# Holding the gating layer's first z weights in an idle buffer, and running a second u and z pair ahead of the last spatial product

## The chip, the cores and the metric

The kernel runs on the 8 cores of one Trainium2 chip. Each core has its own prompt stream of 4096 frames and four of the 32 sample streams; the cores exchange nothing and run the same program. The metric is the device time in microseconds (us) of the slowest core. TensorE multiplies, VectorE (DVE) and ScalarE (ACT) work on elements and bring results out of PSUM, GpSimd (POOL) does a few copies, and SyncE (SP) issues nearly all DMA transfers, in the order of its queue.

## What is computed

The reference is a trunk of four layers over rows of 1024 numbers, with an inner width of 2048:

```python
for i in range(DEPTH):                       # kinds 0, 1, 2, 0
    h = rmsnorm(x, norm_g[i])
    if kind == 0:   # pooling mixer on u, then (y * silu(z)) @ pool_out_w
        ...
    elif kind == 1: # GLU, causal depthwise convolution of width 31, layernorm, silu
        ...
    else:
        p = h @ sgu_in_w[j]                                    # (B,T,3E)
        u, v, z = p[..., :D_INNER], p[..., D_INNER:2 * D_INNER], p[..., 2 * D_INNER:]
        y, st = sgu_mixer(u, v, sgu_w[j], sgu_b[j], sgu_norm_g[j], sgu_norm_b[j])
        out = (y * jax.nn.silu(z)) @ sgu_out_w[j]
    x = x + out
```

The third layer, the gating layer, is the one that changes. Its mixer normalises v (layernorm over the 2048 channels), multiplies it along the 128 positions of a chunk by a lower-triangular matrix of each of four heads (the *spatial product*), adds a bias, and multiplies by u.

## The kernel before

Each core walks through eight groups (g = 0 to 7) of 512 prompt frames. In the even groups 32 frames of a sample stream come along, so that a group has 544 columns. Activations lie with channels on partitions and frames along the row, in bf16 for TensorE (`h`, `ym`) and in f32 for the residual. In a group the four layers follow one another: L0 (pooling), L1 (convolution), L2 (gating), L3 (pooling).

**Weights.** A pass over the layers uses 112 chunks of 128 x 2048 bf16 (512 KB). They stream through nine buffers, `slots`: chunk `gi` lies in slot `gi % 9`. `use_chunk` issues loads on SyncE up to six chunks ahead. In group 0 a chunk comes from `wst` as f32 (1 MB) through one of two staging buffers `stg` (L238), is converted on ScalarE (L240) and stored by ScalarE's queue in `wq` (L244); later groups load it from `wq` (L269). In an input projection one chunk holds the columns of two output tiles, `m2` = 0 and 1.

**Order.** The order of instructions on every engine is that in which the program adds them (`S.add`); semaphores are worked out from what each reads and writes. So a DMA on SyncE or a conversion on ScalarE that has to wait holds up all that was added to that engine behind it.

**The gating layer.** Its chunks are 8 of v (offsets 0 to 7 from 56), then u and z in turn: chunk 8 is u's first, 9 z's first (the diff calls it `L2 + 9`), 10 u's second, and so on, then 8 of the output projection. The eight v chunks stay in their slots until the last block of frames is done; with chunk 8 all nine slots are full, so chunk 9 takes the slot of the first v chunk. The frames go in blocks of 128 (four, and a fifth of 32 sample frames in even groups). For a block, `vstage` runs the v projection (L1050) into four PSUM banks; ScalarE brings it out (L1062); DVE takes statistics (L1067, L1070); two small ScalarE steps and two DVE steps make scale and shift (L1072 to L1081); ScalarE normalises (L1085). In the sample block, and in the last block of g = 7, L1090 normalises once more in f32 for the output, and in the sample block SyncE stores that in `svn` (L1096). `sstage` runs the spatial product (L1108, 16 matmuls, four to a head, each head in a bank of its own); DVE evicts three heads (L1133, four instructions each) and ScalarE the fourth (L1119). The loop is `vstage(t+1)`, `sstage(t)`.

Ahead of the last `sstage` stand early projections that `pre_tile` makes (L554): in even groups the u tile of channel tile 0, in odd groups its u and z tiles. PSUM has eight banks; a tile is two banks in even groups and one in odd groups; `vtiles` lists the eight in the order of the ring, the spatial product uses the first four, the early tiles the next ones. Then, for the 16 channel tiles, come the rest of u and z (L382), each z through Silu on ScalarE (L1225), two DVE products (L1228, L1231) and so into `ym` for the output projection (L484, L382, residual added at L500).

**The buffer.** `wdt` (three parts of 128 x 1024 bf16) holds the diagonal matrices of the convolution in L1, and in group 0 and in the last group some data of the pooling layers. In L2 nothing uses it. `L433` makes the row scale for the next layer; in L2 of group 0 DVE also works out `bt`, the bias of the spatial product (L1153), once.

## Time and profile before

| | us |
|---|---|
| median of 3 runs (4903.69 to 5186.77) | 4910.05 |
| the profiled execution | 4896.68 |
| its span, first to last instruction, slowest core (core 5) | 4895.1 |
| TensorE busy in it | 3990.6 (82%) |
| DVE, ScalarE, GpSimd busy | 2111.9, 1860.0, 648.3 |
| spans of the eight cores | 4868.6 to 4895.1 |
| granted TensorE clock, mean of a core | 0.928 to 0.933 |

"Busy" counts time in which at least one instruction of the engine was at work. The granted clock is the share of full speed (2.4 GHz) that TensorE was given; it is 0.5 or 1.0 at any moment. Shapes in a row read partitions x elements. All rows are of core 5. A row's figure in brackets is the idle time of the engine just before it, and behind the arrow what ended it.

### The profile page before, as it was taken

To read this page: it belongs to the slowest core of one execution; us is meant where nothing else is said; L and a number is where in the kernel's file an instruction comes from. 1 tells how busy PE (TensorE), PEld (TensorE's weight loads), DVE (VectorE), ACT (ScalarE), POOL (GpSimd) and SP (SyncE) were. 2 spreads that over 40 slices of the span, in tenths; PEclk is the share of its full clock that TensorE was granted. 3 is DMA by queue.
4 is the path that set the end of the run, shared out by engine and by line. 5 is a ranking of instruction groups with operands and counts; after the bars stand their busy time and mean duration, and the time that the engine had idled before them with its cause. 6 is when DMAs were issued, how large, how long until landed. Compare 5 with 4: busy or idle time off the path is not lost.

```text
span 4895.1 us, 88633 instructions; the slowest of 8 cores (4868.6 to 4895.1 us)
## 1 busy us (share of the span) xinstructions
PE 3990.6 (82%) x30572; PEld 2529.7 (52%) x30572; DVE 2111.9 (43%) x4227; ACT 1860.0 (38%) x3353; POOL 648.3 (13%) x931
## 2 busy tenths in 40 slices
PE   3845657778899878998899878997899878978886
PEld 1533445533345757753446657753446667733443
DVE  2411333542347334552457234552556234542444
ACT  3522645432434244332534243331524243332523
POOL 1111000211002210112002200212012200202000
PEclk8977879989999999999999999999999999999999
DMA  6754547645345543445254643446254633446353
GB/s 192 259 176 142 202 160 272 231 149 157 116 152 167 141 124 103 143 152 155 93 184 156 149 118 102 142 153 161 104 171 156 152 102 112 138 181 162 112 178 140
DMA packets 320997, 752.98 MB, mean 154 GB/s; under 512 B 85680, under 2 KB 171056, under 8 KB 302512
## 3 DMA queue, kind: packets, MB, share of 16 engines
q1 hardware_dynamic: 304432, 688.59, 45.7%
q10 hardware_dynamic: 16128, 58.73, 2.9%
q8 instruction: 254, 4.16, 0.4%
q14 instruction: 183, 1.50, 0.1%
HBM read 647.62 MB, written 99.56 MB: 153 GB/s over the span
## 4 chain that ended last, share of the span: by engine, by line
PE 65%; DVE 10%; ACT 9%; DMA 8%; issue 7%; SPq 1%; ACTq 1%; POOL 0%; DVEq 0%; POOLq 0%
PE ps L382 45%; DMA stg<-wst 6%; PE ps L837 5%; PE ps L484 5%; DVE h L453 3%; ACT slots L240 2%; PE ps L554 2%; ACT t L858 2%; PE ps L1050 2%; PE ps L421 1%; PE ps L1009 1%; PE ps L394 1%; PE ps L865 1%; DVE big L1133 1%; DVE big L847 1%
## 5 line engine op out<-in xcount | busy, mean ns | idle before, releaser
L382 PE MATMUL ps<-h,slots 128*128 128x272 bf16 (+1 forms) x12448 | 1964.8, 319 | 171.5 <-ACT t L880 48.4
L382 PEld LDWEIGHTS ps<-h,slots 128*128 128x128 bf16 x12448 | 1230.8, 100 | 874.3 <-issue 251.6
L382 PE MATMUL ps<-ym,slots 128*128 128x272 bf16 (+1 forms) x4352 | 671.9, 313 | 16.3 <-DVE x L500 16.3
L382 PEld LDWEIGHTS ps<-ym,slots 128*128 128x128 bf16 x4352 | 430.4, 99 | 231.1 <-issue 27.2
L806 POOL TENSOR_TENSOR wdt<-par,bc 128x1024 bf16<-128x1024 f32 x128 | 244.5, 1910 | 1075.1 <-PE ps L837 656.5
L654 ACT ACTIVATE scr<-ps,par 128x272 f32<-128x272 f32 (+3 forms) x495 | 209.7, 477 | 302.7 <-PE ps L382 158.9
L484 PE MATMUL ps<-ym,slots 128*128 128x272 bf16 (+1 forms) x1792 | 291.8, 323 | 12.2 <-DVE t L1228 7.3
L847 DVE TENSOR_SCALAR big<-ps,par 128x276 f32<-128x276 f32 (+1 forms) x192 | 106.8, 584 | 445.9 <-PE ps L837 445.9
L776 DVE TENSOR_TENSOR agb<-ps,t 128x272 bf16<-128x272 f32 (+3 forms) x256 | 98.7, 429 | 449.7 <-ACT t L762 439.7
L837 PE MATMUL ps<-ym,wdt 128*32 128x276 bf16 (+2 forms) x6144 | 271.5, 328 | 16.5 <-DMA ym<-asc 16.1
L762 ACT ACTIVATE t<-ps 128x272 f32<-128x272 f32 (+1 forms) x164 | 69.4, 458 | 565.5 <-PE ps L382 556.5
L865 PE MATMUL ps<-t,ones_e 128*128 128x272 bf16 (+1 forms) x192 | 50.9, 320 | 283.3 <-ACT t L858 283.3
L240 ACT ACTIVATE slots<-stg 128x2048 bf16<-128x2048 f32 x96 | 183.4, 1911 | 205.0 <-DMA stg<-wst 184.9
L500 DVE TENSOR_TENSOR x<-ps,x 128x272 f32<-128x272 f32 x256 | 99.2, 436 | 345.6 <-PE ps L382 285.1
L484 PEld LDWEIGHTS ps<-ym,slots 128*128 128x128 bf16 x1792 | 175.7, 98 | 123.8 <-issue 15.5
L1228 DVE TENSOR_TENSOR t<-ps,t 128x272 f32<-128x272 f32 (+1 forms) x192 | 94.9, 522 | 335.1 <-ACT t L1225 335.1
L1225 ACT ACTIVATE t<-ps 128x272 f32<-128x272 f32 (+1 forms) x192 | 82.2, 462 | 366.7 <-PE ps L382 364.9
L837 PEld LDWEIGHTS ps<-ym,wdt 128*32 128x32 bf16 x6144 | 165.2, 100 | 107.8 <-issue 59.3
L500 DVE TENSOR_TENSOR stg<-ps,stg 128x512 f32<-128x512 f32 x128 | 84.9, 689 | 315.1 <-PE ps L382 226.7
L602 POOL COPY scr<-pool_hp 128x15 f32<-128x15 f32 x256 | 130.5, 511 | 612.6 <-DVE t L706 348.6
L1050 PE MATMUL ps<-slots,scr 128*128 128x256 bf16 (+1 forms) x1792 | 210.4, 280 | 0.0
L631 ACT ACTIVATE big<-ps 128x272 f32<-128x272 f32 (+1 forms) x362 | 154.7, 464 | 145.2 <-PE ps L382 137.4
(132 smaller groups left out, 4422.3 us busy)
## 6 DMA issues: line engine op xcount, KB each, us to landing
slots<-wq SPq DMA_DIRECT2D x784, 512.0 KB, 4.3
stg<-wst SPq DMA_DIRECT2D x120, 1024.0 KB, 7.2
ym<-asc SPq DMA_DIRECT2D x512, 129.8 KB, 3.6
wq<-slots ACTq DMA_DIRECT2D x112, 512.0 KB, 7.1
asc<-agb SPq DMA_DIRECT2D x128, 128.0 KB, 3.7
yT<-big SPq DMA_DIRECT2D x64, 256.0 KB, 2.2
x<-wun SPq DMA_DIRECT2D x16, 1024.0 KB, 5.9
x<-xT SPq DMA_DIRECT2D x32, 256.0 KB, 5.7
```

Of the source, the lines that this page charges most:

```text
L240: S.add("act", lambda e, st=st, out_ap=out_ap: e.activation(out=out_ap, in_=stg[:, st, :], func=AF.Copy), reads=[("stg", st)], writes=out_ ...
L382: inst = e.matmul(psap(tile, bi, n), lhsT=lhs_fn(k), rhs=rhs_fn(k, c0, n), start=(k == 0), stop=(k == nk - 1))
L453: S.add("dve", lambda e, k=k: e.scalar_tensor_tensor(out=h[:, k, a:T], in0=XAP(G, k, a, T - a), scalar=par[:, g0 + k: g0 + k + 1], in1=rs[ ...
L484: inst = e.matmul(psap(tile, bi, n), lhsT=slots[:, sl, k * 128:(k + 1) * 128], rhs=ym[:, k, c0:c0 + n], start=(ki == 0), stop=(ki == 15))
L500: blockwise("dve", G, lambda e, bi, c0, n, m=m, tile=tile: e.tensor_tensor(out=XAP(G, m, c0, n), in0=psap(tile, bi, n), in1=XAP(G, m, c0, ...
L602: S.add("pool", lambda e: e.tensor_copy(out=seqb[:, p, 0:H], in_=pool_hp[:, j, ct, :]), reads=[("pool_hp", j, ct)], writes=[("seqb", p)])
L631: blockwise("act", G, lambda e, bi, c0, n, ct=ct, tile=tile: e.activation(out=big[:, ct, c0:c0 + n], in_=psap(tile, bi, n), func=AF.Silu), ...
L654: inst = e.activation(out=seqb[:, p, so:so + ln], in_=psap(tile, bi, ln, off=lo - c0), func=AF.Copy, scale=par[:, P_PSCALE + j * 16 + ct:P ...
L806: S.add("pool", lambda e, w2=w2, wc=wc: e.tensor_tensor(out=wdt[:, w2, :].rearrange("p (a b) -> p a b", b=32), in0=wc.unsqueeze(2).broadca ...
L837: inst = e.matmul(psap(tile, bi, n, p0=32 * gq, p1=32 * gq + 32), lhsT=wdt[:, w2, (gq * 8 + k) * 32:(gq * 8 + k) * 32 + 32], rhs=ash[b][:, ...
L847: inst = e.tensor_scalar(out=big[:, ct, c0:c0 + n], in0=psap(tile, bi, n), scalar1=par[:, P_CONVB + ct:P_CONVB + ct + 1], scalar2=None, op ...
L1050: inst = e.matmul(psap(tile, bi, 256, p0=0, p1=nt, off=c2 * 256), lhsT=xg[:, k, tok0:tok0 + nt], rhs=slots[:, slv[cc], k * 256:(k + 1) * 256],
```

## The change

Chunk `L2 + 9`, z's first, no longer takes a slot but the first two parts of `wdt`; so it can be loaded while all eight v chunks are held. Its slot stays empty for that turn. `use_chunk` may run one chunk further ahead while the v chunks are held. Ahead of the last spatial product there are now u and z of channel tile 0 in even groups (banks 6 and 7 serve the z tile), and u and z of channel tiles 0 and 1 in odd groups. Behind it the ring of PSUM tiles starts again at `vt0` in both.

```diff
+    def slot_of(gi):
+        return NSLOT if gi % NCH == L2 + 9 else gi % NSLOT
+
+    def SLOT(sl):
+        return slots[:, sl, :] if sl < NSLOT else wdt2d[:, 0:2048]
+
+    def SLK(sl):
+        return [("slot", sl)] if sl < NSLOT else [("wdt", 0), ("wdt", 1)]
...
     def use_chunk(gi, hold_from=None):
         upto = min(gi + PF, total_chunks - 1)
         if hold_from is not None:
-            upto = min(upto, hold_from + NSLOT - 1)
+            upto = min(upto, hold_from + NSLOT - 1 + (hold_from % NCH == L2))
...
             if tci == nch - 1:
                 table(AF.Silu)
-                if even:
-                    mk, rd, tile = pre_tile(G, gbase + cbase + 8, 0, tuple(q[0] for q in vtiles[4:6]), h)
-                    upre["u"] = tile
+                units = [(0, "u"), (0, "z")] if even else [(0, "u"), (0, "z"), (1, "u"), (1, "z")]
+                for q, (c, nmz) in enumerate(units):
+                    tile = tuple(b[0] for b in vtiles[4 + 2 * q:6 + 2 * q]) if even else vtiles[4 + q]
+                    mk, rd, tile = pre_tile(G, gbase + cbase + (8 if nmz == "u" else 9), c, tile, h)
+                    upre[nmz, c] = tile
                     S.add("pe", lambda e, mk=mk: mk(e, range(8)), reads=rd + HALL, writes=[*PK(tile)])
-                else:
-                    for q, nmz in ((4, "u"), (5, "z")):
-                        mk, rd, tile = pre_tile(G, gbase + cbase + (8 if nmz == "u" else 9), 0, vtiles[q], h)
-                        upre[nmz] = tile
-                        S.add("pe", lambda e, mk=mk: mk(e, range(8)), reads=rd + HALL, writes=[*PK(tile)])
-                    nxt_tile = (vt0 + 6) % len(G["tiles"])
                 state["tile"] = 0
             sstage(tci)
-        state["tile"] = vt0 if even else nxt_tile
+        state["tile"] = vt0
...
-                if ct == 0:
-                    tU = upre["u"]
+                if ("u", ct) in upre:
+                    tU = upre["u", ct]
```

All other places that read or write a slot by its number go through `SLOT` and `SLK`. The early tiles show in the order of the engines. TensorE in group 0, the end of the gating layer's loop, before and now; the line numbers of the changed kernel are higher by 9 (1108 is 1117, 554 is 563, 382 is 391):

```order
L1050 MATMUL ps<-slots,scr 32x256 x64
L1108 MATMUL ps<-wmT,ym 128x128 x16
L554 MATMUL ps<-h,slots 128x272 x16
L1108 MATMUL ps<-wmT,dbuf 128x32 x16
L382 MATMUL ps<-h,slots 128x272 x496
```

```order
L1059 MATMUL ps<-slots,scr 32x256 x64
L1117 MATMUL ps<-wmT,ym 128x128 x16
L563 MATMUL ps<-h,slots 128x272 x16
L563 MATMUL ps<-h,wdt 128x272 x16
L1117 MATMUL ps<-wmT,dbuf 128x32 x16
L391 MATMUL ps<-h,slots 128x272 x16
L391 MATMUL ps<-h,wdt 128x272 x16
L391 MATMUL ps<-h,slots 128x272 x448
```

The z tile of channel tile 0 has moved in front of the last 16 small products, and the z tiles of channel tiles 0 and 1, both from chunk 9, now read `wdt`. In group 1, without a sample block, the same place before and now:

```order
L1108 MATMUL ps<-wmT,ym 128x128 x16
L554 MATMUL ps<-h,slots 128x512 x16
L1108 MATMUL ps<-wmT,dbuf 128x128 x16
L382 MATMUL ps<-h,slots 128x512 x240
L484 MATMUL ps<-ym,slots 128x512 x48
```

```order
L1117 MATMUL ps<-wmT,dbuf 128x128 x16
L1059 MATMUL ps<-slots,scr 128x256 x64
L1117 MATMUL ps<-wmT,ym 128x128 x16
L563 MATMUL ps<-h,slots 128x512 x8
L563 MATMUL ps<-h,wdt 128x512 x8
L563 MATMUL ps<-h,slots 128x512 x8
L563 MATMUL ps<-h,wdt 128x512 x8
L1117 MATMUL ps<-wmT,dbuf 128x128 x16
```

Sixteen more matmuls stand in front of the last products, and 224 instead of 240 behind them. ScalarE in group 0, where the row scale for the gating layer is made (L433, now L442), before and now:

```order
L240 ACTIVATE slots<-stg 128x2048
L244 DMA wq<-slots 128x2048
L433 ACTIVATE rs<-ps,epsb 128x272 x2
L436 ACTIVATE rs<-rs 128x544
L1062 ACTIVATE vraw<-ps 128x512 x4
```

```order
L240 ACTIVATE slots<-stg 128x2048
L253 DMA wq<-slots 128x2048
L240 ACTIVATE wdt<-stg 128x2048
L253 DMA wq<-wdt 128x2048
L442 ACTIVATE rs<-ps,epsb 128x272 x2
L445 ACTIVATE rs<-rs 128x544
L1071 ACTIVATE vraw<-ps 128x512 x4
```

The conversion of z's first chunk has moved here, in front of the row scale, from behind the eviction of the last spatial product. On SyncE, in group 2, the load has moved in front of the store of `svn`; before and now:

```order
L988 DMA o_convs<-cso 128x480
L269 DMA slots<-wq 128x2048 x11
L1096 DMA svn<-vraw 32x2048
L269 DMA slots<-wq 128x2048 x31
L1296 DMA stg<-xT 128x512 x8
```

```order
L997 DMA o_convs<-cso 128x480
L278 DMA slots<-wq 128x2048 x11
L278 DMA wdt<-wq 128x2048
L1105 DMA svn<-vraw 32x2048
L278 DMA slots<-wq 128x2048 x30
L1301 DMA stg<-xT 128x512 x8
```

Of the 31 chunk loads behind the store 30 are left, u's second chunk first among them.

## Rows read from the trace of the kernel before

**Rows 1.** The page: busy time of TensorE, and the chain that ended last.
```profile
PE 3990.6 (82%) x30572; PEld 2529.7 (52%) x30572; DVE 2111.9 (43%) x4227; ACT 1860.0 (38%) x3353; POOL 648.3 (13%) x931
...
PE 65%; DVE 10%; ACT 9%; DMA 8%; issue 7%; SPq 1%; ACTq 1%; POOL 0%; DVEq 0%; POOLq 0%
```

**Rows 2.** Timeline, g = 2: start, duration (us), engine, line, instruction, count, [idle before].
```profile
1910.45 1.07 PE L1108 MATMUL ps<-wmT,ym 128*128 128x128 bf16 x16
1911.37 2.01 PE L554 MATMUL ps<-h,slots 128*128 128x272 bf16 x16
...
1917.22 2.09 ACT L1090 ACTIVATE vraw<-vraw,mv 32x2048 f32<-32x2048 f32 x1
...
1917.38 0.39 PE L1108 MATMUL ps<-wmT,dbuf 32*128 32x32 bf16 x8 [4.00 <-ACT dbuf L1085]
...
1920.42 11.63 SPq L269 DMA_DIRECT2D slots<-wq  x9
...
1920.46 0.26 PE L1108 MATMUL ps<-wmT,dbuf 32*128 32x32 bf16 x4 [1.96 <-ACT big L1119]
...
1925.03 7.21 PE L382 MATMUL ps<-h,slots 128*128 128x272 bf16 x37 [4.31 <-DMA slots<-wq]
```

**Rows 3.** Windows, g = 2: PE, PEld, DVE, ACT, POOL busy; clock, DMA, GB/s.
```profile
1917.30:1920.70 3.40, 0.89 (x16) 0.68 (x16) 2.69 (x16) 3.38 (x6) 0.24 (x1) 0.50 0.18 39
...
1925.00:1930.70 5.70, 5.67 (x26) 3.71 (x27) 0.89 (x3) 0.69 (x2) 0.00 (x0) 0.50 1.01 398
...
1937.00:1987.00 50.00, 49.68 (x417) 39.61 (x415) 19.69 (x39) 8.91 (x26) 0.00 (x0) 1.00 0.41 130
```

**Rows 4.** Timeline of ScalarE, g = 2: the Silu of z0, z1 and z2.
```profile
1928.91 0.69 ACT L1225 ACTIVATE t<-ps 128x272 f32<-128x272 f32 x2 [6.03 <-PE ps L382]
1933.61 0.69 ACT L1225 ACTIVATE t<-ps 128x272 f32<-128x272 f32 x2 [4.01 <-PE ps L382]
1937.45 0.69 ACT L1225 ACTIVATE t<-ps 128x272 f32<-128x272 f32 x2 [3.15 <-PE ps L382]
```

**Rows 5.** Timeline, g = 1.
```profile
1371.67 3.62 PE L554 MATMUL ps<-h,slots 128*128 128x512 bf16 x16
...
1375.08 6.29 DVE L1133 SCALAR_TENSOR_TENSOR big<-ps,par,bt 128x128 f32<-128x128 f32 x24
...
1377.57 1.85 PE L1108 MATMUL ps<-wmT,dbuf 128*128 128x128 bf16 x16 [2.29 <-ACT dbuf L1085]
...
1379.22 11.06 PE L382 MATMUL ps<-h,slots 128*128 128x512 bf16 x46
...
1383.90 0.60 ACT L1225 ACTIVATE t<-ps 128x512 f32<-128x512 f32 x1 [2.45 <-PE ps L382]
```

**Rows 6.** Windows, g = 1, columns as in rows 3.
```profile
1377.50:1381.20 3.70, 3.63 (x21) 2.21 (x22) 3.70 (x15) 3.67 (x11) 1.27 (x2) 0.54 0.03 7
```

**Rows 7.** Timeline and one window, g = 7.
```profile
4663.58 0.59 PE L1108 MATMUL ps<-wmT,dbuf 128*128 128x128 bf16 x4 [1.70 <-ACT big L1119]
...
4669.78 0.60 ACT L1225 ACTIVATE t<-ps 128x512 f32<-128x512 f32 x1 [3.24 <-PE ps L382]
...
4661.40:4668.20 6.80, 5.10 (x18) 2.09 (x18) 4.25 (x14) 5.11 (x12) 2.37 (x2) 0.50 0.00 0
```

**Rows 8.** Timeline, g = 0: ScalarE and DVE at the row scale, TensorE later on.
```profile
626.35 0.87 ACT L433 ACTIVATE rs<-ps,epsb 128x272 f32<-128x272 f32 x2 [0.51 <-PE ps L421]
...
631.83 2.06 ACT L1062 ACTIVATE vraw<-ps 128x512 f32<-128x512 f32 x4 [3.87 <-PE ps L1009]
...
632.07 4.23 DVE L1153 SCALAR_TENSOR_TENSOR bt<-ps,par,bc 128x128 f32<-128x128 f32 x16 [29.62 <-PE ps L1144]
...
715.55 3.68 PE L382 MATMUL ps<-h,slots 128*128 128x272 bf16 x16 [20.02 <-ACT big L1119]
...
754.19 7.70 PE L382 MATMUL ps<-h,slots 128*128 128x272 bf16 x64 [1.75 <-DVE t L1228]
```

**Rows 9.** DMA issues from 682.5 to 791.9: count, size, median us to landing.
```profile
stg<-wst SPq DMA_DIRECT2D x23, 1024.0 KB, 7.6
```

More of the change, by code:

```diff
@@ L241, in raw_load @@
               reads=[("stg", st)], writes=out_keys)
+    def slot_of(gi):
[4 more added lines that the diff above has]
+        return [("slot", sl)] if sl < NSLOT else [("wdt", 0), ("wdt", 1)]
     def store_chunk(ci, sl):
-        S.add("act", lambda e, ci=ci, sl=sl: [e.dma_start(out=wq[ci], in_=slots[:, sl, :])],
-              reads=[("slot", sl)], writes=[("wq", ci)], dkey=("slot", sl))
+        S.add("act", lambda e, ci=ci, sl=sl: [e.dma_start(out=wq[ci], in_=SLOT(sl))],
+              reads=SLK(sl), writes=[("wq", ci)], dkey=("slot", sl))
     def pool_part(ci):
@@ L255, in issue_load @@
         grp = gi // NCH
-        sl = gi % NSLOT
+        sl = slot_of(gi)
         if grp == 0:
@@ L265, in issue_load @@
                 idx = ci + 4 if ci < L3 else 92 + ci - L3 + 4
-            raw_load(idx, slots[:, sl, :], [("slot", sl)])
+            raw_load(idx, SLOT(sl), SLK(sl))
             store_chunk(ci, sl)
         else:
-            S.add("sp", lambda e, ci=ci, sl=sl: [e.dma_start(out=slots[:, sl, :], in_=wq[ci])],
-                  reads=[("wq", ci)], writes=[("slot", sl)], dkey=("slot", sl))
+            S.add("sp", lambda e, ci=ci, sl=sl: [e.dma_start(out=SLOT(sl), in_=wq[ci])],
+                  reads=[("wq", ci)], writes=SLK(sl), dkey=("slot", sl))
     def raw_issue(j, gq):
@@ L368, in use_chunk @@
             state["loaded"] += 1
-        return gi % NSLOT
+        return slot_of(gi)
     L0 = 0
@@ L393, in fn @@
                     for bi, (c0, n) in enumerate(G["blocks"]):
-                        inst = e.matmul(psap(tile, bi, n), lhsT=slots[:, sl, k * 256 + m2 * 128: k * 256 + m2 * 128 + 128],
+                        inst = e.matmul(psap(tile, bi, n), lhsT=SLOT(sl)[:, k * 256 + m2 * 128: k * 256 + m2 * 128 + 128],
                                         rhs=h[:, k, c0:c0 + n], start=(k == 0), stop=(k == 7))
                     return inst
-                S.add("pe", fn, reads=[("slot", sl), *HKEY(k)], writes=[*PK(tile)])
+                S.add("pe", fn, reads=SLK(sl) + HKEY(k), writes=[*PK(tile)])
             return
         mm_tile(G, tile, 8,
-                lambda k: slots[:, sl, k * 256 + m2 * 128: k * 256 + m2 * 128 + 128],
+                lambda k: SLOT(sl)[:, k * 256 + m2 * 128: k * 256 + m2 * 128 + 128],
                 lambda k, c0, n: h[:, k, c0:c0 + n],
-                reads=[("slot", sl)] + HALL)
+                reads=SLK(sl) + HALL)
     def blockwise(eng, G, fn_block, reads, writes):
@@ L553, in mk @@
                 for bi, (c0, n) in enumerate(G["blocks"]):
-                    inst = e.matmul(psap(tile, bi, n), lhsT=slots[:, sl, k * 256 + m2 * 128: k * 256 + m2 * 128 + 128],
+                    inst = e.matmul(psap(tile, bi, n), lhsT=SLOT(sl)[:, k * 256 + m2 * 128: k * 256 + m2 * 128 + 128],
                                     rhs=src[:, k, c0:c0 + n], start=(k == 0), stop=(k == 7))
             return inst
-        return mk, [("slot", sl)], tile
+        return mk, SLK(sl), tile
     def ps_scale(G, out_fn, tile, writes, scalar=None):
@@ L1217, in sgu_layer @@
                     inproj(G, slu, m2, tU)
-                if ct == 0 and "z" in upre:
-                    tZ = upre["z"]
+                if ("z", ct) in upre:
+                    tZ = upre["z", ct]
                 else:
```

## The prediction

> **What bounds the kernel now.** I read the page first. TensorE is busy for 3990.6 of 4895.1 us, 82%; no other engine passes 43% [rows 1]. The chain that ended last is TensorE for 65% of the span, by far the largest part of it L382, the input and output projections. So a microsecond in which TensorE stands idle is worth about a microsecond, as long as the work that it is waiting to do is on the chain. The change acts at one place of each of the eight groups: around the last spatial product (L1108) of the gating layer and the u and z projections (L382) behind it. So the next view was the timeline there, for each kind of group, and the windows, for the granted clock.
>
> A group with a sample block (g = 2, 4, 6; shown g = 2) [rows 2]. TensorE ends the early u tile (L554) at 1913.38 and is idle 4.00 us, until ScalarE has normalised the last v block (L1085). Its sixteen small products then dribble until 1920.73: the last four wait 1.96 us for an eviction (L1119) which on ScalarE stands behind L1090, 2.09 us that make the output copy of v. Then it is idle again, 4.31 us, until a weight chunk lands. Why so late: SyncE works its queue in order, the store of `svn` waits for L1090, and all weight chunks from z0 on stand behind that store; they go out at 1920.42. From 1917.3 to 1930.7 the clock is at 0.50, behind that at 1.00 (shown from 1937.0 on) [rows 3]. ScalarE's Silu gives the ends of the z tiles: z0's at 1928.91, z1's at 1933.61, z2's at 1937.45 [rows 4]. The first tile, 1925.03 to 1928.91, took 3.88 us at half clock; the last two, 1933.61 to 1937.45, took 3.84 together, so a tile of 16 matmuls costs 1.92 at full clock.
>
> A group without one (g = 1, 3, 5; shown g = 1) [rows 5]. The early u and z tiles take 3.62 us together; then 2.29 idle for the normalised block; the sixteen products last until 1379.4; L382 follows at once, at 1379.22. No load is waited for. u1 and z1 end when the Silu starts at 1383.90. From 1377.5 to 1381.2 the clock is at 0.54, half speed but for an edge [rows 6].
>
> The last group (g = 7) is like it, but the last products also wait 1.70 us for the eviction behind L1090, L382 starts right behind them, at 4664.0, and its first two tiles end at 4669.78; the clock is 0.50 up to 4668.2 [rows 7].
>
> Group 0 loads weights as f32, 1 MB each at 7.6 us from issue to landing, converts each on ScalarE (L240) and stores it. Six conversions stand on ScalarE in front of the eviction of the last spatial product, and TensorE waits 20.02 us for it. From there on L382 stands still for 1.8 to 3.6 us in each round of four tiles (7.70 us), always because the Silu stands behind conversions that wait for a landing [rows 8, 9]. That stretch is bound by the stream of loads: 23 of them in the 109.4 us from 682.5 to 791.9, 4.76 us each.
>
> **The change, part by part.**
>
> *The buffer.* z's first chunk goes to `wdt`, whose last readers, the diagonals' matmuls, ended in the layer before; it is issued in front of `svn`, with some 45 us to go, where the others take 4.3 us. No bytes are added and no wait falls on TensorE. What is queued behind it: on SyncE the `svn` store, far off. In group 0 its conversion and store stand on ScalarE in front of L433, which makes the scale of the rows. L433 now starts at 626.35, right behind a conversion. One more load cannot start before a staging buffer is free, some 4 us before that; it lands 7.6 later, near 630, and the conversion is another 2, so L433 starts near 632. Who waits: L1169 on TensorE and L1062 on ScalarE, which stands at 631.83 after 3.87 idle, so becomes late by up to 2 us. Behind it the statistics on DVE wait anyway, as DVE is busy with `bt` until 636.30 [rows 8]. I cost this at 0; without that cover it is 2 us, once.
>
> *Sample groups, three of them.* z0 (1.92) moves into the 4.00 idle in front of the products, which start when they did. Behind them u1 and z1 need no landing, since a chunk holds two tiles' columns and both chunks are there; they start at 1920.73, not 1925.03. Their PSUM: u1 takes two banks that DVE evicts; z1's second bank is evicted by ScalarE (1.1 us, behind L1090 and a table load), while u1 runs. What is late next is the chunk of u2, now first in the line at 1920.42: landed at 1925.0, as z0's was. u1 and z1 cost 3.84 at full clock and 7.76 at half. The idle is shorter by nearly 6 us, so full clock comes back earlier. I take u1 at half (ends 1924.6) and z1 between the two (2.9, ends 1927.5). Before, z1 ended at 1933.6. Gain 6.1. Bounds: all at full clock, u2 begins at the landing, 1925.0, gain 8.6; half clock right to 1930.7, both end at 1928.5 and u2's next 2.2 us count half, which leaves 5.1 - 1.1 = 4.0; and 1 us more for a second chunk that is not there in time, 3.0. Three groups: 18.3 (9 to 25.8).
>
> *Groups without sample, three.* The second pair costs 3.62 and begins at 1375.29, so it ends at 1378.9; the products could have begun at 1377.57. They are 1.3 late and no longer wait for evictions, so they take 1.07 as where nothing hinders them [rows 2] and not 1.85: they end at 1380.0. New wait: u2 now takes the bank that the first of them wrote, not one that is free. Four evictions of 0.27 each on DVE from 1379.3 make it free at 1380.4. Before, u2 began at 1383.9. Gain 3.5 with full clock throughout. If the half clock comes as it did, from 1377.5 to 1381.2, it lies on 1.4 us of the pair, 1.07 of products and the start of u2, which costs up to 1.8: gain 1.7. I take 2.7 (the nearer row is one with 2.29 idle ahead; here some 0.4 is left). Three groups: 8.1 (5.1 to 10.5).
>
> *The last group.* The pair ends at 4661.8 or 4662.0, the products still wait for the eviction, until 4663.58, and u2 starts at 4664.2 instead of 4669.78. At half clock until 4668.2 it does 2.0 us less than at full: gain 5.4 down to 3.4; I take 4.3.
>
> *Group 0.* One load leaves the bound stretch: the six conversions in front of the eviction are those of the next six chunks, and one fewer follows. u1 runs early where z0 did; what starts at 715.55 is z1 and no longer u1. Worth one place of the stream, 4.76; I take 5, from 3 (later idle swallows some) to 7 (the first Silu no longer stands behind a seventh conversion).
>
> *PSUM order.* The ring of tiles is a place or two further on in each later stage. A tile at a change of ring then meets a bank used one or two turns earlier or later; at some 0.4 us for an eviction and a few such places per group I cost it at 0, within 3 us either way.
>
> Sum: 18.3 + 8.1 + 4.3 + 5 = 35.7 us less; from 9 + 5.1 + 3.4 + 3 = 20.5 to 25.8 + 10.5 + 5.4 + 7 = 48.7. The profiled execution took 4896.68, 1.6 beside its span, so it would be 4861.0. The other runs gave 4903.69, 4910.05 and 5186.77; the last is 5.6% off the rest and left out. The middle of the three that are left is 4903.69, and I forecast from that: 4868.
>
> **A rule weighed against a row.** Sixteen matmuls of 512 columns took 3.62 us, 226 ns each [rows 5]. By the Trainium skill ("TensorE: Matmul & The Clock Gate", Back-to-back issue gap) a stream of weight load and matmul settles near 131 ns at that size. By that figure, an estimate, the second pair would be 2.1 us, hide wholly in the 2.29 idle, and be worth 2.1 in such a group in place of my 2.7, so 1.8 less in the sum. The row decides.
>
> **The rivals.**
> (a) *The clock no longer falls.* For it: the half clock comes each time behind an idle stretch and ends after TensorE has been busy [rows 3, 6]; idle goes from 4.0 + 2.4 + 4.3 to about 2.0 + 2.4 in sample groups and from 2.29 to near 0.4 in the others. Against: the products themselves are thin (0.89 busy of 3.40), and in sample groups they still dribble. It gives the upper end, 48.7: 4855. The same page (Part 1) calls the throttled state the default that activity releases; the rows agree as far as they go.
> (b) *The gain is only half there*, because u1 and z1 meet another wait in the place of the old: half clock to its old end, the second chunk late, the odd groups' idle filled but the products late. The lower end, 20.5, or a little less: 4885.
> (c) *It ends slower.* TensorE works on more, and thinner, stretches of full and half clock: the pair in front, run just before a fall, no longer keeps the clock up behind the products, so a fall comes a second time in L382. One fall as that of rows 7 (0.50 up to 4668.2 from 4661.4) costs 3.4 us of work. Two more in each of eight groups cost 54, against 35.7 gained: 18 slower, 4922. It decides from 4.5 us lost per group. Against it: behind the products L382 was busy 49.68 of 50 us at 1.00 [rows 3], and nothing in it is thinned.
> (d) *It does not do what it says*: the early chunk is there, but TensorE is not what the end hangs on and the time comes back in a later stage. Against: 65% of the chain is TensorE. Nearly no change, 4900.
>
> **How the numbers follow.** Forecast as summed: 0.55, time 4868 (4858 to 4880). (a) 0.17, 4855. (b) 0.18, 4885. (c) 0.04. (d) 0.06. The range 4845 to 4892 takes in the forecast, (a), (b) and the 0.15% by which those three runs differ from their middle; it leaves out (c), (d) and some spill. 2% of this kernel is 98 us, about what a measurement can tell from no change; no case but a gross surprise reaches it. Faster by over 2%: 0.02; within: 0.95; slower: 0.03.
>
> **What would show it.** Right: in g = 2 no wait of L382 for `slots<-wq` over 0.5 us, L382 from 1920.7 on in that group's time, the products at the same distance from the last v matmuls as before; in g = 1 idle before the products near 0 and a wait of a few tenths for L1133 before u2; in g = 0 L433 some 5 us later and L382 to its end about 5 us sooner. Wrong: the products of g = 2 start later than their normalised block, L382 waits for a chunk at u2 or z2, or the half clock lasts as long behind L382's start as it did (5.7 us). What would make the forecast wrong most of all is the clock, since each fall more or less in a group is worth 1.7 to 3.4 us.

## The result, and the profile after

The changed kernel against the kernel before, run in turn on one chip: ratio 0.9936, 95% interval 0.992 to 0.9952, so 0.64% less time (0.48 to 0.80%). The forecast, 4868 against a middle of 4903.69, was 0.73% less. The median of all six timed runs is 4951.43 us (4868.80 to 5087.15), outside the forecast range of 4845 to 4892, and that of the kernel before 5048.41 (4903.69 to 5494.93): both are pulled up by runs in which the four cores of a die had a lower granted clock than the others, as in the 5186.77 that the prediction left out, and such runs, and in the profiles below such cores, are left out of every comparison. The other three runs of the changed kernel gave 4868.80, 4875.14 and 4883.44, inside that range, those of the kernel before 4903.69, 4905.57 and 4910.05. Their middles are 30.4 us apart; 35.7 were forecast. The profiled execution took 4875.14, against 4896.68.

The page of the changed kernel, the lines that answer to [rows 1]:

```profile
PE 3986.7 (82%) x30377; PEld 2537.2 (52%) x30572; DVE 2111.5 (43%) x4227; ACT 1858.5 (38%) x3353; POOL 647.4 (13%) x931
...
PE 66%; DVE 9%; ACT 9%; DMA 7%; issue 7%; SPq 1%; ACTq 1%; POOL 0%; DVEq 0%; another core or an unknown queue 0%; POOLq 0%
```

Nothing else has become the bound. All rows from here on are of core 5 where no other is named, and every line number is higher by 9 (by 5 behind L1200). The timeline of g = 2, TensorE and SyncE, which answers to [rows 2]:

```profile
1886.83 1.07 PE L1117 MATMUL ps<-wmT,ym 128*128 128x128 bf16 x16
1887.74 2.01 PE L563 MATMUL ps<-h,slots 128*128 128x272 bf16 x16
1889.60 2.02 PE L563 MATMUL ps<-h,wdt 128*128 128x272 bf16 x16
1893.76 0.37 PE L1117 MATMUL ps<-wmT,dbuf 32*128 32x32 bf16 x8 [2.15 <-ACT dbuf L1094]
...
1896.84 0.26 PE L1117 MATMUL ps<-wmT,dbuf 32*128 32x32 bf16 x4 [1.97 <-ACT big L1128]
1897.07 3.49 PE L391 MATMUL ps<-h,slots 128*128 128x272 bf16 x16
1900.40 2.02 PE L391 MATMUL ps<-h,wdt 128*128 128x272 bf16 x16
1902.25 4.00 PE L391 MATMUL ps<-h,slots 128*128 128x272 bf16 x32
...
1896.80 4.65 SPq L278 DMA_DIRECT2D slots<-wq  x9
```

From the early u tile to L391 it was 13.66 us (1911.37 to 1925.03); it is 9.33 (1887.74 to 1897.07), with one tile more done in it. The idle in front of the products has shrunk from 4.00 to 2.15, as they now wait behind a z tile; the 1.96 for the eviction has stayed; the 4.31 for the chunk is gone. u1 takes 3.3 us, z1 1.9, and the loads that now go out at 1896.80 are there when u2 needs them.

The windows, which answer to [rows 3] and [rows 6]:

```profile
1893.50:1897.00 3.50, 0.78 (x16) 0.66 (x16) 2.87 (x16) 3.39 (x7) 0.16 (x1) 0.96 0.18 42
1897.00:1901.00 4.00, 4.00 (x26) 2.82 (x23) 0.95 (x3) 2.60 (x8) 1.44 (x2) 0.61 0.90 297
1901.00:1906.00 5.00, 5.00 (x45) 4.05 (x43) 2.08 (x4) 0.69 (x2) 0.00 (x0) 1.00 1.03 418
1359.60:1408.10 48.50, 48.48 (x225) 22.03 (x226) 22.43 (x38) 9.66 (x19) 1.18 (x1) 1.00 0.46 141
```

The clock (the last figure but two) fell at 1917.3 before, at the start of the products, and came back between 1930.7 and 1937. Now it holds until the last four of them (0.96 over the stretch), falls there and is back at 1.00 by 1901, 4 us after L391 began. The last row is the whole of L391 in g = 1: never below full speed. The timeline that answers to [rows 5], g = 1:

```profile
1350.94 1.89 PE L563 MATMUL ps<-h,slots 128*128 128x512 bf16 x8
...
1356.12 1.89 PE L563 MATMUL ps<-h,wdt 128*128 128x512 bf16 x8
1357.85 1.06 PE L1117 MATMUL ps<-wmT,dbuf 128*128 128x128 bf16 x16
1359.62 4.69 PE L391 MATMUL ps<-h,slots 128*128 128x512 bf16 x21 [0.71 <-DVE big L1142]
```

Four early tiles fill the wait for the normalised block; the products take 1.06 and are not waited for. u2 waits 0.71 for the bank that the first product wrote. It starts 8.7 us behind the first early tile; before, that was 12.2 [rows 5]. In g = 7 the last products still wait for the eviction behind the second normalisation, 1.27 us in place of 1.70 [rows 7]:

```profile
4617.18 0.83 PE L1117 MATMUL ps<-wmT,dbuf 128*128 128x128 bf16 x12
4619.28 0.38 PE L1117 MATMUL ps<-wmT,dbuf 128*128 128x128 bf16 x4 [1.27 <-ACT big L1128]
4619.52 6.85 PE L391 MATMUL ps<-h,slots 128*128 128x512 bf16 x31
```

Group 0, ScalarE, DVE and TensorE, against [rows 8]:

```profile
621.08 1.91 ACT L240 ACTIVATE wdt<-stg 128x2048 bf16<-128x2048 f32 x1 [4.55 <-DMA stg<-wst]
623.49 0.87 ACT L442 ACTIVATE rs<-ps,epsb 128x272 f32<-128x272 f32 x2 [0.51 <-ACT wdt L240]
...
621.96 4.23 DVE L1162 SCALAR_TENSOR_TENSOR bt<-ps,par,bc 128x128 f32<-128x128 f32 x16 [26.42 <-PE ps L1153]
...
626.95 2.47 DVE L1076 BATCH_NORM_STATS2 bst<-vraw 128x6 f32<-128x512 f32 x4
...
625.25 1.17 PE L1178 MATMUL ps<-epsb,rs 1*128 1x1 f32 x10 [3.40 <-ACT rs L445]
...
681.57 2.01 PE L391 MATMUL ps<-h,slots 128*128 128x272 bf16 x16 [1.31 <-DVE big L1142]
704.31 3.78 PE L391 MATMUL ps<-h,wdt 128*128 128x272 bf16 x16 [20.73 <-ACT big L1128]
```

**The ledger.** To see where the time went I cut each trace into stages, from the first TensorE instruction of one to the first of the next, and took the mean over the cores. The gating layer from its v projection to the start of its output projection, after less before, in us; "forecast" are the terms of the prediction:

| group | 0 | 1 | 2 | 3 | 4 | 5 | 6 | 7 | sum |
|---|---|---|---|---|---|---|---|---|---|
| measured | -5.6 | -2.8 | -6.5 | -3.0 | -6.4 | -3.2 | -5.7 | -5.5 | -38.8 |
| forecast | -5 | -2.7 | -6.1 | -2.7 | -6.1 | -2.7 | -6.1 | -4.3 | -35.7 |

In g = 0 the cores lie far apart (159.5 to 170.0 us for the changed kernel), so its -5.6 is good to some 2.6 us; the others agree far better. All that lies outside these stages came out 11 us longer in this pair of traces. That was not forecast, and some of the experiments are on it. For them I also split a stage's loss in two: TensorE's idle, and its half-speed loss, which is half of the time that it was busy at 1.2 GHz. The gating layer's -38.9 is idle 137.7 to 108.7 (-29.0) and half-speed loss 39.6 to 30.1 (-9.5). The rest: idle 713.7 to 710.7, half-speed loss 149.2 to 164.8.

### The profile page after: what moved, and what is told of

Its sections match the earlier page's. It is cut to its first block, busy times and chain, and to the rows that moved or that the text cites. A ratio compares the mean times of both kernels' runs of the same rounds, so it can differ in the third digit from the quotient of the medians.

```text
span 4873.6 us, 88400 instructions; the slowest of 8 cores (4839.0 to 4873.6 us)
## 1 busy us (share of the span) xinstructions
PE 3986.7 (82%) x30377; PEld 2537.2 (52%) x30572; DVE 2111.5 (43%) x4227; ACT 1858.5 (38%) x3353; POOL 647.4 (13%) x931
## 4 chain that ended last, share of the span: by engine, by line
PE 66%; DVE 9%; ACT 9%; DMA 7%; issue 7%; SPq 1%; ACTq 1%; POOL 0%; DVEq 0%; another core or an unknown queue 0%; POOLq 0%
PE ps L391 45%; DMA stg<-wst 6%; PE ps L846 5%; PE ps L493 5%; DVE h L462 3%; PE ps L563 2%; ACT slots L240 2%; PE ps L1059 2%; ACT t L867 2%; PE ps L403 1%; PE ps L430 1%; PE ps L1018 1%; PE ps L874 1%; DVE big L1142 1%; DVE big L856 1%
## 5 line engine op out<-in xcount | busy, mean ns | idle before, releaser
L391 PE MATMUL ps<-h,slots 128*128 128x272 bf16 (+1 forms) x12154 | 1929.3, 319 | 168.0 <-ACT t L889 48.2
L391 PEld LDWEIGHTS ps<-h,slots 128*128 128x128 bf16 x12256 | 1213.3, 100 | 829.2 <-issue 213.7
L391 PE MATMUL ps<-ym,slots 128*128 128x272 bf16 (+1 forms) x4327 | 674.3, 313 | 18.3 <-DVE x L509 16.6
L391 PEld LDWEIGHTS ps<-ym,slots 128*128 128x128 bf16 x4352 | 431.7, 99 | 235.1 <-issue 33.2
L771 ACT ACTIVATE t<-ps 128x272 f32<-128x272 f32 (+1 forms) x164 | 69.4, 458 | 572.6 <-PE ps L391 561.9
L681 POOL COPY pool_hp<-scr 128x15 f32<-128x15 f32 x224 | 143.4, 640 | 509.8 <-ACT scr L663 487.5
```

Of the source, the lines that this page charges most:

```text
L391: inst = e.matmul(psap(tile, bi, n), lhsT=lhs_fn(k), rhs=rhs_fn(k, c0, n), start=(k == 0), stop=(k == nk - 1))
L681: S.add("pool", lambda e, p=p, ct=ct: e.tensor_copy(out=pool_hp[:, j, ct, :], in_=seqb[:, p, 512:512 + H]), reads=[("seqb", p)], writes=[( ...
```

## The experiments

Ratios are to the kernel before, from runs in turn on the same chip. "Gating" is the ledger's sum for the gating layer.

**1 and 2: the parts alone.** The buffer, with the early tiles of before, and in the odd groups the place in the ring of before:

```diff
-                units = [(0, "u"), (0, "z")] if even else [(0, "u"), (0, "z"), (1, "u"), (1, "z")]
+                units = [(0, "u")] if even else [(0, "u"), (0, "z")]
...
-        state["tile"] = vt0
+        state["tile"] = vt0 if even else (vt0 + 6) % len(G["tiles"])
```

> The changed kernel with the buffer and the earlier load kept, and the early tiles as they were before (u0 in sample groups, u0 and z0 in the others). Times are of the gating layer (start of its v projection to start of its output projection on TensorE, mean of the cores) against the kernel before; the whole change measured -6.5, -6.4, -5.7 in g = 2, 4, 6; -2.8, -3.0, -3.2 in g = 1, 3, 5; -5.5 in g = 7; -5.6 in g = 0. Theory 1, the gain of a sample group has two parts, the landing that z0 no longer waits for (4.3 idle, less what half clock takes) and z0's 1.9 in the idle ahead of the products: here -4 in each of g = 2, 4, 6, 0 in g = 1, 3, 5, 7 (no load was waited for there), -5 in g = 0 (one load fewer in the bound stretch), -17 in all. Theory 2, the early tiles are the gain and the buffer is only what makes them possible, since z0 without them meets unfinished evictions: -1 at most in sample groups, 0 elsewhere, -3 in all. Theory 3, in g = 0 the load stream is not what counts: 0 there.

And chunk 9 back in its slot, even groups as before, four early tiles in odd ones:

```diff
     def slot_of(gi):
-        return NSLOT if gi % NCH == L2 + 9 else gi % NSLOT
+        return gi % NSLOT
...
-            upto = min(upto, hold_from + NSLOT - 1 + (hold_from % NCH == L2))
+            upto = min(upto, hold_from + NSLOT - 1)
...
-                units = [(0, "u"), (0, "z")] if even else [(0, "u"), (0, "z"), (1, "u"), (1, "z")]
+                units = [(0, "u")] if even else [(0, "u"), (0, "z"), (1, "u"), (1, "z")]
```

> No buffer; z0 in its slot as before; sample groups as before; in the odd groups four early tiles (u0, z0, u1, z1) instead of two. Gating layer against the kernel before, mean of the cores. Theory 1, the odd groups gain by the second pair in the idle ahead of the products alone and need no buffer: -3 in g = 1, 3, 5, -5.5 in g = 7, 0 in the even ones, -14.5 in all. Theory 2, in the odd groups too the earlier load counts: less than half of that.

The buffer alone: 0.996 (0.9943 to 0.9976). Gating: g = 2, 4, 6: -4.4, -4.7, -3.9; g = 0: -7.8; odd groups 0 within 0.3; sum -21.1. Its timeline in g = 2:

```profile
1899.16 2.01 PE L563 MATMUL ps<-h,slots 128*128 128x272 bf16 x16 [0.25 <-ACT vraw L1071]
1905.18 0.39 PE L1117 MATMUL ps<-wmT,dbuf 32*128 32x32 bf16 x8 [4.01 <-ACT dbuf L1094]
...
1908.59 3.71 PE L391 MATMUL ps<-h,wdt 128*128 128x272 bf16 x16
```

The idle of 4 us in front of the products is that of before; L391 follows them without a landing. The odd pair alone: 0.998 (0.9967 to 0.9992); g = 1, 3, 5, 7: -2.8, -2.9, -3.0, -5.1; g = 2, 4, 6 within 0.5; g = 0: -1.6; sum -16.1. So the odd groups owe nothing to the buffer and the sample groups two thirds of theirs; the last third, -6.2 less -4.3, is the z tile moved into the idle.

**3 and 4: what the load waited for.** The `svn` store put on SyncE behind the loads for the early tiles, in the changed kernel (3) and in the kernel before (4), where it is the only edit:

```diff
-                    S.add("sp", lambda e, s=s, VR=VR: [e.dma_start(out=svn[s], in_=VR[0:32, :])],
-                          reads=VK, writes=[("svn",)], dkey=("vraw", bs))
+                    late.append(lambda s=s, VR=VR, VK=VK, bs=bs: S.add(
+                        "sp", lambda e: [e.dma_start(out=svn[s], in_=VR[0:32, :])],
+                        reads=VK, writes=[("svn",)], dkey=("vraw", bs)))
...
                 state["tile"] = 0
+                while late:
+                    late.pop(0)()
             sstage(tci)
```

> The changed kernel, with the store of svn added to SyncE's queue behind the chunk loads of the early tiles instead of in front of them. Gating layer against the changed kernel. Theory 1, with the buffer no chunk is waited for in sample groups, so nothing is to be had there: -0.5 to 0 in g = 2, 4, 6; in g = 0 the two staging loads that stand behind the store start some 40 us earlier, so the conversions begin at once and two fewer loads fall in the bound stretch: -7 to -9.5. Theory 2, g = 0 is held by TensorE and the evictions and not by the stream: 0 to -2 there.

> The kernel before with that same move of the svn store and nothing else. Gating layer against the kernel before. Theory 1, the 4.3 us that TensorE waited for z0 come from the store that stood in front of the load on SyncE: z0 is there when the last products end, so -4 in each of g = 2, 4, 6 as with the buffer alone, -7 to -10 in g = 0, 0 in the odd groups; -20 in all. Theory 2, the slot of the first v chunk is free too late, or the transfers themselves are slow: -1 or less in g = 2, 4, 6.

In the changed kernel: 0.9931 (0.9909 to 0.9953); against it only g = 0 moved, by -4.0, half of what I had put down. In the kernel before: 0.9971 (0.9954 to 0.9987); g = 2, 4, 6: -4.7, -4.2, -4.0; g = 0: -6.3; odd groups 0; sum -19. Its g = 2:

```profile
1893.35 2.01 PE L554 MATMUL ps<-h,slots 128*128 128x272 bf16 x16
1899.37 0.39 PE L1110 MATMUL ps<-wmT,dbuf 32*128 32x32 bf16 x8 [4.01 <-ACT dbuf L1086]
...
1902.95 15.27 PE L382 MATMUL ps<-h,slots 128*128 128x272 bf16 x115 [0.24 <-issue]
```

From the early u tile to L382 9.60 us in place of 13.66, with no new buffer. SyncE's rows show why; first the kernel before, then number 4:

```profile
1919.40 0.33 SPq L1096 DMA_DIRECT2D svn<-vraw  x1
```

```profile
1901.38 0.33 SPq L1098 DMA_DIRECT2D svn<-vraw  x1
1901.87 16.41 SPq L269 DMA_DIRECT2D slots<-wq  x6
```

In the kernel before the store goes out when L1090 has ended (1919.3), and the loads of [rows 2] behind it at 1920.42; in number 4 the load for z0 had gone out by 1891.6, ten us ahead of the store. What the load had waited for was its place behind the store, and the store's own wait for L1090. The buffer did not shorten a transfer; it let one load stand ahead of that store.

**5, 11 and 10: is the give-back real, and what brings it?** The kernel before (5) and the changed kernel (11) once more, unchanged; and the early pair (0, u), (0, z) in every group (10), so that the odd groups are as before:

```diff
-                units = [(0, "u"), (0, "z")] if even else [(0, "u"), (0, "z"), (1, "u"), (1, "z")]
+                units = [(0, "u"), (0, "z")]
...
-        state["tile"] = vt0
+        state["tile"] = vt0 if even else (vt0 + 6) % len(G["tiles"])
```

> The kernel before, once more, to see what a table of stages can tell: mean of the cores, stage by stage, this profile against the first profile of the same kernel. In the runs so far everything outside the gating layer came out 4 to 11 us longer than in that first profile, whichever part of the change was in. Theory 1, the first profile (4896.68) was a short one of its kind (the kernel's median in the second set of runs is 4907.8), and the 11 us that the changed kernel seemed to give back outside the gating layer are that: here the gating layer is the same within 1 in each group and the rest is 5 to 12 longer. Theory 2, they are given back by the change: the rest is the same within 3.

> The changed kernel once more, on the same chip as the two others, so that they are compared side by side. 0.6 to 0.7% faster than the kernel before; gating layer 40 less than before, half speed outside it near 164.

> The buffer and the early z0 of the sample groups, with two early tiles in the odd groups as before. Gating layer against the kernel before. Theory 1, the parts stand side by side, each in its own groups: -6.2 in g = 2, 4, 6, -5 to -7 in g = 0, 0 in g = 1, 3, 5, 7; the buffer alone gave -4.3 in sample groups, so z0 in the idle is worth 2. Half speed outside the gating layer costs 150 us of TensorE's work in the kernel before and 164 in the changed one (a core's mean; half the time that it was busy at half clock), at the same idle; with the odd pair alone 154, with the buffer alone 151. If that goes with the early z0 of sample groups it is 164 here; if with the odd pair, 150.

The kernel before again: gating -0.4, rest +0.8 against the same four cores of its first profile. I had taken it for likely that the first profile was merely a short one; the second did not bear that out. But the timed executions of that kernel that stand beside the experiments have spans of 4887.2 and 4888.5 on average over the cores (8 executions beside numbers 10 and 11, 14 beside 1 to 4), the first profile 4882.0: some 5 of the 11 us may still be that profile. The changed kernel again: 0.9933 (0.992 to 0.9946), gating -38.8, the same; half-speed loss of the rest 162.6. Number 10: 0.9947 (0.9931 to 0.9963), g = 2, 4, 6: -6.0, -6.3, -6.0; g = 0: -3.5, where the buffer alone gave -7.8, so in g = 0 the early z tile costs; odd groups within 0.4; sum -22.4.

Over all kernels run here, the stages outside the gating layer in the traces, means over cores, behind the ± one standard error (95% bounds are about twice as wide):

| | cores | length | idle | half-speed loss |
|---|---|---|---|---|
| early tiles of sample groups as before (before, 5, 4) | 20 | 3959.7 ± 2.7 | 717.6 ± 2.3 | 150.4 ± 1.2 |
| z's first tile early too (changed, 3, 6, 7, 8, 9, 11, 12) | 52 | 3964.6 ± 1.5 | 711.8 ± 1.6 | 162.5 ± 0.7 |
| 10 | 8 | | | 162.5 ± 2.8 |
| odd pair alone (2) | 8 | | | 153.2 ± 2.7 |
| buffer alone (1) | 8 | | | 151.1 ± 1.7 |

So some 12 us of half-speed loss more, which is clear of the noise; 6 of idle less and 5 more of length, which are barely so or not at all. Number 10 has all of the extra half speed, number 1 none of it, and number 2 a quarter, itself not clear of nothing: it comes with the z tile run early in the sample groups. (On cores 4 to 7 number 1 shows a third level of the granted clock beside 0.5 and 1.0, 0.81 for 65 to 92 us of the span; the clock is then not always at one of two levels. It is not counted as half speed here.)

What it costs in time is another matter. The timed executions give the length of the whole pass (mean of the eight cores, less that of the kernel before on the same chip); take the gating layer from it, and the rest is what came back outside:

| | whole pass | gating layer | outside, with 95% bounds |
|---|---|---|---|
| two early tiles in the odd groups: 1 | -21.8 | -21.1 | -0.7 ± 5.7 |
| 4 | -17.1 | -19.0 | 1.9 ± 4.4 |
| 10 | -20.8 | -22.4 | 1.5 ± 5.4 |
| four early tiles there: 2 | -12.5 | -16.2 | 3.6 ± 3.5 |
| 3 | -38.0 | -43.0 | 5.0 ± 5.9 |
| the changed kernel (11) | -31.3 | -38.9 | 7.6 ± 5.2 |
| 12 | -38.0 | -44.3 | 6.2 ± 4.0 |

The first three average 0.9, the other four 5.6, and the difference of 4.7 is good to some 3.8. So the time that comes back goes with the second pair of the odd groups, if with any part, while the extra half speed goes with the z tile of the sample groups: number 10 has all the half speed and kept its gain. Half-speed work that takes the place of idle costs nothing, so the table of half speed is no bill.

What half speed in an unchanged stretch looks like, on core 0: the window is the last output projection of g = 1, the row ahead of it the wait inside it; first in the kernel before,

```profile
1536.67 0.58 PE L421 MATMUL ps<-dbuf,ones_d 128*128 128x512 bf16 x1 [3.32 <-ACT dbuf L507]
...
1513.90:1549.10 35.20, 31.88 (x150) 14.74 (x149) 11.41 (x17) 12.26 (x21) 1.68 (x6) 0.95 0.37 118
```

then in the changed kernel:

```profile
1535.88 0.58 PE L430 MATMUL ps<-dbuf,ones_d 128*128 128x512 bf16 x1 [3.32 <-ACT dbuf L516]
...
1513.10:1549.80 36.70, 33.38 (x149) 15.14 (x148) 11.42 (x17) 12.26 (x21) 1.68 (x6) 0.91 0.34 112
```

Same instructions, same idle of 3.32 us, same work on DVE, ScalarE and GpSimd to 0.01 us; TensorE needs 33.38 in place of 31.88 us, and the granted clock is 0.91 in place of 0.95. The stretch differs from core to core in one kernel too: before it takes 33.8 us on six cores, 35.2 and 35.5 on the others; in the changed kernel 33.8 on one and 35.5 to 36.8 on seven; in number 10 33.8 on seven again. So here it is the whole change that lengthens it, and the extra half speed of number 10 lies elsewhere.

**6: the ring of PSUM tiles.** The changed kernel with the ring moved one place on at the start of L3, so that from there it stands as in the kernel before:

```diff
         S.tag = (g, 'L3')
+        state["tile"] = (state["tile"] + 1) % len(G["tiles"])
```

> The changed kernel, with the ring of PSUM tiles moved one place on at the start of the last pooling layer, so that it stands from there as in the kernel before. Against the changed kernel, mean of the cores. In the changed kernel the last pooling layer of the even groups was 0.5 to 1.0 longer than before, in two profiles, and its output projection in g = 1 and g = 5 by 2. Theory 1, the ring: L3 of g = 0, 2, 4, 6 shorter by 0.5 to 1.0 each and L3o of g = 1, 5 by 1 to 2, some 5 in all. Theory 2, the clock, whose falls lie where they like: no such pattern, each stage within 1 and the idle time of TensorE in them as it was.

The move itself cost 1.8 us in each of g = 2, 4 and 6 (the gating layer's output projection +6.9, L3 -5.1). The last projection of g = 1 and g = 5 came out 0.3 and 1.6 shorter, and the half-speed loss of the rest was 162.8, no less. The give-back is not seen to hang on the ring; a test without a cost of its own I did not find, so this is inconclusive.

**7, 8: the waits that are left.** The f32 normalisation (L1099) moved on ScalarE behind the last eviction, on top of number 3:

```diff
             sstage(tci)
+            if tci == nch - 1:
+                for q in lateact + late:
+                    q()
```

> The kernel with the svn store late, and L1090 too (ScalarE's second normalisation, for the output) added behind the evictions of the last spatial product instead of in front of them. Gating layer against the kernel with the store late alone. Theory 1, the products of a sample group end 2.0 earlier, since the eviction they wait for no longer stands behind L1090's 2.09 us, and u1 follows at once: -1.5 to -2 in g = 2, 4, 6, -1 to -2 in g = 7, -2 in g = 0, 0 in g = 1, 3, 5; -8 in all. Theory 2, the time goes into the next wait (the first Silu, or z1's bank, which that late L1090 now holds up): -0.5 at most in each.

Against number 3 the sample groups moved by -1.6, -1.2 and -2.2, g = 7 by nothing, where I had expected -1 to -2, g = 0 by +2.9, where I had expected -2: worth having in g = 2, 4, 6 alone. And in g = 0 the last spatial product in front of the early tiles:

```diff
                 table(AF.Silu)
+                if g == 0:
+                    state["tile"] = 0
+                    sstage(tci)
                 units = [(0, "u"), (0, "z")] if even else [(0, "u"), (0, "z"), (1, "u"), (1, "z")]
```

> The changed kernel, with the last spatial product of group 0 added in front of the early tiles and their six conversions. That takes away the wait of 20 us of TensorE for an eviction behind those conversions. g = 0 against the changed kernel. Theory 1, the stretch is bound by the stream of loads and conversions, and that wait costs nothing: 0 to -1.5 in the gating layer. Theory 2, the wait is on the path: -5 or more.

g = 0 came out 1.4 us longer than in the changed kernel, which is no difference: on the same four cores the changed kernel itself came out 2.5 longer the second time (number 11). Its timeline there:

```profile
693.20 2.02 PE L391 MATMUL ps<-h,slots 128*128 128x272 bf16 x16
695.05 2.02 PE L391 MATMUL ps<-h,wdt 128*128 128x272 bf16 x16
721.52 7.83 PE L391 MATMUL ps<-h,slots 128*128 128x272 bf16 x48 [24.45 <-DVE t L1238]
```

The 20.73 us wait is gone, and one of 24.45 stands a tile later. That group is bound by its stream of loads, as the prediction took it to be; the wait of 20.73 us costs nothing.

**9 and 12: put together.** The changed kernel, the store late in all sample groups, L1099 late in g = 2, 4, 6 only; 12 is 9 once more:

```diff
+                (lateact.append if g > 0 and nt == 32 else lambda q: q())(lambda nt=nt, VR=VR, VK=VK, bs=bs: S.add("act", lambda e: e.activation(
...
                 state["tile"] = 0
+                while late and g == 0:
+                    late.pop(0)()
             sstage(tci)
+            if tci == nch - 1:
+                for q in lateact + late:
+                    q()
```

> The changed kernel with the svn store late in every sample group, and L1090 late in g = 2, 4, 6 alone (late L1090 gave 1.2 to 2.2 in those and cost 3 in g = 0). Gating layer against the changed kernel, undisturbed cores: -1.2 to -2.2 in g = 2, 4, 6, -3 to -5 in g = 0, 0 in the odd groups, -9 in all, 0.2% of the time, so at the edge of what the timing can tell; against the kernel before 0.8 to 0.9% faster. Theory 2, the parts do not add up (the late store in g = 2, 4, 6 now holds up a weight chunk): less than -4 in all.

> The kernel with both moves (svn store late, L1090 late in g = 2, 4, 6) once more, for its time, since too few executions of it agreed the first time. Its gating layer was 7.4 us less than the changed kernel's in the profiles and 46 less than before's. If the time follows the profiles, 0.8% to 1.0% faster than the kernel before (the changed kernel: 0.67%); if what the gating layer gains comes back as half speed elsewhere, as with the early z0, 0.6 to 0.7%.

Number 9 gave a profile (4855.83) and no ratio that can be used; against the changed kernel g = 0 -5.0, g = 2, 4, 6: -0.7, -1.1, -0.7, sum -7.4, so the sample groups gave less than the 1.2 to 2.2 expected. Number 12: 0.9925 (0.9909 to 0.994), between its two forecasts; gating -44.3 against the kernel before, and -5.4 against the changed kernel, where number 9 had -7.4. Its g = 2:

```profile
1903.24 2.01 PE L563 MATMUL ps<-h,slots 128*128 128x272 bf16 x16 [0.25 <-ACT vraw L1073]
...
1909.26 0.37 PE L1120 MATMUL ps<-wmT,dbuf 32*128 32x32 bf16 x8 [2.15 <-ACT dbuf L1096]
1910.12 0.56 PE L1120 MATMUL ps<-wmT,dbuf 32*128 32x32 bf16 x8 [0.48 <-DVE big L1145]
1911.38 3.79 PE L391 MATMUL ps<-h,slots 128*128 128x272 bf16 x16 [0.70 <-DVE big L1145]
```

The 1.97 for the eviction is gone; from the early pair to L391 8.14 us in place of 9.33. It is the shortest of the versions run, though its interval overlaps that of the changed kernel.

## Why the prediction was right, and the step that failed

*What bounds the kernel.* Right: TensorE's share of the chain is 66%, and where idle and half speed went out of the gating layer the layer became shorter by nearly their sum (38.5 of 38.9).

*The buffer.* Cost 0, right in the main, and for the reason given. Its conversion pushed L442 from 0.95 us behind the last small product of the row scale (L421 625.40, L433 626.35) to 8.2 (615.30 and 623.49), 7 later where 5 were forecast. TensorE waits 3.40 us at L1178, but DVE is busy with `bt` until 626.2: from that product to the statistics it is 11.65 us, before 11.22. All of g = 0 ahead of its early tiles became 0.9 us longer. That is near enough to 0.

*Sample groups.* 6.2 on average against 6.1. Both halves stand apart in the runs: 4.3 for the landing (numbers 1 and 4), 1.9 for the tile in the idle, the 1.92 of [rows 4]. The products began and L391 followed as worked out: 9.33 us behind the early u tile, where 1920.73 less 1911.37, 9.36, were forecast. u1 and z1 took 5.4 us to z1's Silu:

```profile
1902.51 0.69 ACT L1230 ACTIVATE t<-ps 128x272 f32<-128x272 f32 x2 [2.67 <-PE ps L391]
```

6.8 were forecast, 7.76 would be all at half speed. So g = 2 on core 5 gained 7.8 us; the other cores gained 5.6 to 7.1 there, as on cores 0 to 4 more half speed fell ahead of the place, and on cores 6 and 7 less had lain behind it before. On core 0 the fourth block's v projection, the same 64 matmuls behind the same idle, took 8.58 us in the kernel before,

```profile
1888.90 0.38 PE L1108 MATMUL ps<-wmT,ym 128*128 128x128 bf16 x4 [2.74 <-DVE big L1133]
...
1891.64 8.58 PE L1050 MATMUL ps<-slots,scr 128*128 128x256 bf16 x64
```

and in the changed kernel 9.49:

```profile
1889.18 0.38 PE L1117 MATMUL ps<-wmT,ym 128*128 128x128 bf16 x4 [2.75 <-DVE big L1142]
...
1892.05 9.49 PE L1059 MATMUL ps<-slots,scr 128*128 128x256 bf16 x64
```

So on core 5 the forecast for u1 and z1 was 1.4 us too dear, and nothing stood in it for the clock ahead of the place, which took some of that back on other cores. Over all cores and the three groups the errors are smaller: ahead of the early u tile +0.1 (+0.6, +0.1, -0.4 in g = 2, 4, 6) where nothing was forecast, from it to L391 -4.1 where -4.3 was, behind it -2.3 where -1.8 was. In g = 2 the half clock around the place lasted 13.7 us on six cores before and 10.3 on two; now it lasts 6.9 on seven and 3.4 on core 5.

*Groups without sample.* 3.0 against 2.7. "If the half clock comes as it did" did not come true inside L382: from its start to the output projection it was 52.76 us in g = 1 on core 5 and is 48.34 now, on every core; the 16 matmuls that left it are 3.45 of the 4.4, the other 1.0 is half speed that is gone. On core 5 g = 1 gained 3.3; on cores 1 and 3 the stretch ahead of L391 is 1.6 us longer than on the others (40.81 against 39.19), which brings the mean to 2.8.

The four early tiles start 1.73 us apart, 216 ns a matmul, and the clock was at 1.00 there; the 131 ns of the Trainium skill ("TensorE: Matmul & The Clock Gate", Back-to-back issue gap) are not seen, the row was the better guide, and the pair did not hide wholly in the 2.29 us.

*Last group and g = 0.* 5.5 against 4.3, a little over the upper bound of 5.4: TensorE's half-speed time in that group's gating layer went from 7.4 to 2.6 us, mean of the cores, and L391 itself is at 1.00 throughout (53.9 us before on core 5, 48.34 now), which is rival (a) for this one place. 5.6 against 5 in g = 0, which is luck in part: the buffer alone gave 7.8 there (number 1), above the upper bound of 7, and the early z tile took 2 to 4 of it back (number 10, the changed kernel), which was not forecast.

*The step that failed* is "PSUM order", costed "at 0, within 3 us either way", and with it the silent assumption that stages outside the gating layer keep their time and their clock. The gating layer gave 38.9 us where 35.7 were forecast; the whole pass gave 31.3 in number 11, so 7.6 us came back outside (2.4 to 12.8). Settled is this much: the traces of both kernels repeat (5, 11); half-speed loss outside grew by some 12 us, at unchanged idle and work in single stretches (core 0 above), and it comes with the z tile run early in the sample groups (10 has it, 1 and 4 do not). Not settled is which part costs the time, since number 10 lost nothing that can be told from 0 and the kernels with four early tiles in the odd groups lost 3.6 to 7.6; nor why the clock falls more often there. The only trial on the ring (6) did not bring it back, so the cause stays open.

*The rivals.* (a) holds in L391 of the odd groups and of g = 7, and halfway in the sample groups; (b) is refuted by the ledger for the gating layer; (c), more falls and slower, had more half speed in mind and in the wrong place: it came outside L382, 12 us of it and not 54, and not all of that is time; (d) holds for some 8 of 39 us (± 5): time did come back in other stages, though TensorE is what the end hangs on.

## What to carry to other kernels

When TensorE waits for a load, look first at what stands ahead of that load on the queue that issues it: here moving one store gave half of the gain of the whole change (0.9971 against 0.9936) and no buffer was needed. A projection tile moved into an idle stretch is worth its full length only if what it stood in front of does not start later. And forecast the whole pass, since a change in one layer moved falls of the clock in others: here 3.6 to 7.6 us came back outside the layer in the kernels with the second pair, so some 0.1 to 0.2% is the room to keep, an estimate from this kernel alone. Count it in time and not in half speed, of which some only takes the place of idle.

## What the runs showed that I had not expected

- The granted clock of a stretch is not set by that stretch alone: same instructions, same 3.32 us idle, 0.95 and 0.91. It differs between the cores of one kernel too, yet the sum repeats: over 52 core traces the half-speed loss outside the changed layer is 162.5 us, over 20 of the other kind 150.4, with standard errors of 0.7 and 1.2; so the sum goes with the program and not with chance.
- The fall comes late: in g = 2 the clock was 0.96 during the 3.5 us in which TensorE was busy for 0.78, and 0.61 in the 4.0 us behind them in which it was busy throughout. The half-speed price of an idle stretch was paid here by what followed it.
- TensorE's wait of 20.73 us in g = 0 cost nothing (number 8 removes it, and the group is no shorter).
